# Conformer convolution's LayerNorm in two column ranges, with the latent range and the latent rows handled beside the first projection tile

## The chip, the cores and the metric

One NeuronCore of a Trainium2 chip runs the whole program. The metric is the device time of one execution in microseconds. Engines are named as in the profile: PE is TensorE (PEld its weight loads), DVE is VectorE, ACT is ScalarE, POOL is GpSimd, SP is the engine whose queue issues most of the DMAs.

## What is computed

A two-layer backbone over 256 context tokens and 512 latent tokens of width 1024. Layer 0 mixes tokens by a convolution module, layer 1 by windowed attention; each layer ends in a top-2 mixture of 16 experts. The change touches the end of layer 0's convolution module and the start of the step that follows it.

```python
def layernorm(x, g, b):
    x32 = x.astype(jnp.float32)
    mu = jnp.mean(x32, axis=-1, keepdims=True)
    xc = x32 - mu
    var = jnp.mean(xc * xc, axis=-1, keepdims=True)
    return (xc * lax.rsqrt(var + EPS) * g.astype(jnp.float32) + b.astype(jnp.float32)).astype(x.dtype)

def conformer_conv(h, pw1, pw1_b, dw, dw_b, ln_g, ln_b, pw2, pw2_b):
    u = h @ pw1 + pw1_b
    u = u[..., :D_MODEL] * jax.nn.sigmoid(u[..., D_MODEL:])
    half = (CONV_WIDTH - 1) // 2
    u = depthwise_conv(u, dw, dw_b, (half, half))
    u = jax.nn.silu(layernorm(u, ln_g, ln_b))
    return u @ pw2 + pw2_b
...
        xl = xl + mod_l[2] * yl
...
            xc = xc + mod_c[2] * yc
            hc2 = modulate(rmsnorm(xc, norm_ffn[i]), mod_c[3], mod_c[4])
            y2 = moe(jnp.concatenate([hc2, hl2], axis=1), *moe_prm)
```

`mod_l` and `mod_c` are the modulation vectors of the latent and the context stream: index 2 is the gate on the mixer's output, 3 and 4 are shift and scale of the norm before the experts.

## The kernel before, in words

**Layout.** The convolution's result lies transposed: `V` (storage AR) has the 1024 channels as 8 blocks of 128 partitions and, for each, `CONVW` = 783 columns: the 256 context tokens, some columns between, and the 512 latent tokens. The normalisation over channels is a sum over partitions and blocks, so PE makes it with a matrix of ones: the mean into `MEAN`, the sum of squares into `VAR` (both in PSUM).

**End of the convolution block** (lines 1360 to 1380 on DVE, 1278 to 1290 on ACT). DVE subtracts the mean (L1368), ACT squares each block (L1282), PE sums the squares (L1246). Then one chain runs over all 783 columns: DVE makes variance plus epsilon into `STD` (L1374), ACT takes the root (L1284), DVE the reciprocal (L1377), DVE multiplies each of the 8 blocks by it (L1380), and ACT applies Silu with the channel's gain and bias (L1287). Each Silu raises `z_ready`, on which the projection's matmuls wait (`wait0`).

`STD` has no storage of its own: it lies in row 3 of `ROWS`, a tile of six rows of 1024 numbers, broadcast to all partitions. Rows 0, 1, 2 are to hold the context stream's gate, scale and shift; rows 3, 4, 5 those of the latent stream. They are written by `load_row` (L468) out of `rows_of_layer`, a small array in HBM that is itself written late, by two DMAs (L464).

**Projection and routing** (`project_and_route`, from L751). Six tiles of 128 tokens, two of context and four of latents. For each tile PE makes two halves of 512 columns (`h` = 0, 1; L858, 8 channel blocks each, two instructions for a block). DVE multiplies a half by the gate row (L975) and adds it to the residual `X` (L978): `add_half`. Halves of `X` are then transposed by PE (L800) for the router, ACT and DVE take the squares' sum and the norm, DVE writes the scaled and shifted tile (L1048, L1053), and `choose` picks the experts. In program order PE asks for DVE's first half of tile `i` (`x_new`) before the transposes that stand after the fourth block of its second half. The bias of the projection times the gate is made once for each stream into `GB` (L1061, storage RING) and added to `X` ahead of the tile's halves (`bias_x`, L1037).

**Order of the queues.** Everything is written out by hand, in one list of instructions for each engine. SP's list at this place: the projection's bias row (L1157 to L1186 stand before it, the load of the second pointwise weights), the two writes of `rows_of_layer`, then a wait for `rows_out` and for all 8 products of L1380 (`scaled`), the six row loads, the first expert weights (L708), eight clearing writes of an output array (L782), and the tiles' results (L786). DVE waits for all six rows (`rows_in`) before it does anything of the projection.

```python
                sp.wait_ge(rows_out, 32)
                if L == 0:

                    sp.wait_ge(scaled, KT)
                for s in streams:
                    for v, w in zip((2, 4, 3), row[s]):
                        load_row(sp, L, s, v, w, rows_in[L])
```

Of the kernel before, what the change touches and what calls it, by code (L numbers as in the profile page):

```python
# [16 lines left out]
ALU = mybir.AluOpType  # L17
ACT = mybir.ActivationFunctionType
# [106 lines left out]
def build(nc, a, out):  # L125
    with ExitStack() as stack:
# [621 lines left out]
            st(V_.tensor_scalar(CUM[:, 0, :], const("iota")[:, 0:NE], float(deep), None, ALU.mult))  # L748
            dve_n[0] = st.n

        def project_and_route(block, L, lhs, weights, bias, tiles, lhs_wait):  # L751


            NT = len(tiles)
# [10 lines left out]
            @block.sync  # L765
            def _(sp):

                sp.wait_ge(rows_out, 32)
                if L == 0:

                    sp.wait_ge(scaled, KT)
                for s in streams:
                    for v, w in zip((2, 4, 3), row[s]):
                        load_row(sp, L, s, v, w, rows_in[L])
                load_weight(sp, L, 0, 1)
                load_weight(sp, L, 0, 3)
                if L == 1:
                    load_weight(sp, L, 1, 1)
                    load_weight(sp, L, 1, 3)
                sp.wait_ge(nil_set[L], 1)  # L780
                for b in range(MINB[L] // 2, MAXB[L] // 2):
                    sp.dma_start(yd[L][b * P:(b + 1) * P, :].rearrange("p (a n) -> p a n", a=4),  # L782
                                 NIL.unsqueeze(1).to_broadcast([P, 4, 256])).then_inc(nil_out[L], 16)
                for i in range(NT - 1):
                    sp.wait_ge(h2_ready[L], i + 1)
                    sp.dma_start(h2d[L][i * P:(i + 1) * P, :], H2[:, i % 2, :]).then_inc(h2_out[L][i % 2], 16)  # L786
                sp.wait_ge(y_summed[L], 2 * NT)
                sp.wait_ge(x_new[L], 2 * NT - 1)
                load_weight(sp, L, L + 1, 1)
                load_weight(sp, L, L + 1, 3)  # L790
                load_weight(sp, L, 0, 2)
                for b in range(2):
                    sp.wait_ge(h2_out[L][b], 16 * (NT // 2))
                sp.wait_ge(nil_out[L], 16 * (MAXB[L] - MINB[L]) // 2)

            @block.tensor
            def _(pe):
# [52 lines left out]
                for i in range(NT):  # L850
                    u = i - 1
                    for h in range(2):
                        if i >= 2:
                            pe.wait_ge(y_used[L], 2 * (i - 2) + h + 1)
                        for k in range(KT):
                            if i == 0 and h == 0:
                                lhs_wait(pe, k)
                            ins = pe.matmul(PS[:, 2 * (i % 2) + h, :], lhs(i, k),  # L858
                                            weights(k)[:, h * 512:(h + 1) * 512],
                                            start=(k == 0), stop=(k == KT - 1))  # L860
                            if u >= 0 and h == 0 and k == 1:
# [101 lines left out]
            def _(dve):  # L963
# [91 lines left out]
                if L == 1:  # L1055
                    router_tables(dve, L, streams)
                    st.n = dve_n[0]
                dve.wait_ge(rows_in[L], 16 * 3 * len(streams) + (16 if bias is not None else 0))
                if bias is not None:
                    for s in streams:  # L1060
                        st(V_.tensor_tensor(GB[:, s, :], bias, ROWS[:, row[s][0], :], ALU.mult))  # L1061
                    bias_x(0)
                for i in range(NT):
                    t = tiles[i]
                    u = i - 1
                    add_half(i, 0)
                    if i:
                        choose(u)
                    add_half(i, 1)
                    if i:  # L1070
                        read_rank(u)
                    dve.wait_ge(xB_turned[L], i + 1)
                    V_.tensor_copy(XTB[:, i % 2, 4:8, :], PS[:, 5, :].rearrange("p (k n) -> p k n", k=4)).then_inc(
                        xB_copied[L], 1)
                    dve.wait_ge(f_sq[L], 2 * i + 2)
                    V_.scalar_tensor_tensor(out=ss[:, t:t + 1], in0=ss_half[:, 0, t:t + 1], scalar=EPS,
                                            in1=ss_half[:, 1, t:t + 1], op0=ALU.add, op1=ALU.add).then_inc(f_ms[L], 1)
                    if i:
                        destinations(u, u + 1)
                    norm_scale(i)  # L1080
                    if i == 0:
                        dve.wait_ge(shift_summed[L], 1)
                        s0 = streams[0]
                        V_.tensor_copy(CST[:, s0:2, :],
                                       SHIFT[:, s0 * NE:2 * NE].rearrange("p (s e) -> p s e", e=NE)).then_inc(
                                           shift_ready[L], 1)
                        dve.wait_ge(shift_ready[L], 1)
                    scale_h2(i)
                    shift_h2(i)
                    if bias is not None and i < NT - 1:  # L1090
                        bias_x(i + 1)
                choose(NT - 1)
# [48 lines left out]
        BROW = RING[:, 0, 0:D]  # L1141
        GB = RING[:, 0, D:3 * D].rearrange("p (s n) -> p s n", s=2)
        STD = ROWS[:, 3, 0:CONVW]
        MEAN = PSF[:, 0:CONVW]
        VAR = PSF[:, 1024:1024 + CONVW]
        NSTEP = 2 * (1 + TAPS)
# [10 lines left out]
        with nc.Block() as block:  # L1157
# [93 lines left out]
            def _(act):  # L1251
# [26 lines left out]
                for f in range(KT):  # L1278
# [1 line left out]
                    if f >= 2:  # L1280
                        act.wait_ge(sq_used, f - 1)
                    nc.scalar.activation(SQ[:, f % 2, :], V[:, f, :], ACT.Square).then_inc(squared, 1)  # L1282
                act.wait_ge(var_ready, 1)
                nc.scalar.activation(STD, STD, ACT.Sqrt).then_inc(std_ready, 1)  # L1284
                for f in range(KT):
                    act.wait_ge(scaled, f + 1)
                    nc.scalar.activation(V[:, f, :], V[:, f, :], ACT.Silu,  # L1287
                                         scale=cols[:, VC["conv_ln_g"] + f:VC["conv_ln_g"] + f + 1],
                                         bias=cols[:, VC["conv_ln_b"] + f:VC["conv_ln_b"] + f + 1]).then_inc(z_ready, 1)

            @block.vector
            def _(dve):
# [78 lines left out]
                    mod_rows_copy(dve, L)  # L1371
                router_tables(dve, 0, (0, 1))
                dve.wait_ge(sq_used, KT)
                nc.vector.tensor_scalar(STD, VAR, 1.0 / D, EPS, ALU.mult, ALU.add).then_inc(var_ready, 1)  # L1374
                dve.wait_ge(std_ready, 1)
                st = Steps(dve, dve_step, dve_n[0])
                st(nc.vector.reciprocal(STD, STD))  # L1377
                for f in range(KT):
                    dve.wait_ge(centred, f + 1)
                    nc.vector.tensor_tensor(V[:, f, :], V[:, f, :], STD, ALU.mult).then_inc(scaled, 1)  # L1380
                dve_n[0] = st.n

            def lhs0(i, k):
                at = i * P if i < CT else LAT0 + (i - CT) * P
                return V[:, k, at:at + P]

            def wait0(pe, k):
                if k == 0:
                    pe.wait_ge(w_in[0], 32)
                pe.wait_ge(z_ready, k + 1)  # L1390

            project_and_route(block, 0, lhs0, lambda k: Wpw2[k // 4][:, k % 4, :], BROW, list(range(TILES)), wait0)


        def load_qkv(sp, c):
# [706 lines left out]
                        nc.scalar.activation(den[:, c], den[:, c], ACT.Exp).then_inc(sink_exp, 1)  # L2102


        def wait1(pe, k):
            if k == 0:
                pe.wait_ge(w_in[1], 32 + 64)
                pe.wait_ge(o_normed, 4 * (LT - 1) + 1)

# [6 lines left out]
        with nc.Block() as block:  # L2116
# [17 lines left out]
            @block.sync  # L2134
            def _(sp):
                o = out[0].rearrange("(t p) d -> t p d", p=P)
                for i, t in enumerate(lat):
                    sp.wait_ge(scaled, KT + i + 1)
                    sp.dma_start(o[i], X[:, t, :]).then_inc(out_sem, 16)
                sp.wait_ge(out_sem, 16 * LT)  # L2140

# [20 lines left out]
```

## Time and profile before

| | |
|---|---|
| median of 3 runs | 1592.72 us (1591.69 to 1592.96) |
| the profiled execution | 1593.22 us, span 1591.4 us |
| busy share of PE, DVE, ACT, POOL | 85%, 48%, 32%, 8% |
| mean granted TensorE clock | 0.927 of full speed |
| bytes moved by DMA | 342.97 MB, mean 216 GB/s |

A busy time is a sum over the span; it does not say which engine sets the pace at a given moment. The trace lists each instruction's start, its duration and, in brackets, how long its engine had been idle before it and whose result ended that idle time. Numbers are microseconds from the span's start unless marked ns. Names are those of the storage: AR is `V`, ROWS is the rows and `STD`, RING holds `GB`, the halves `YT` and the tile `H2`, PS is PSUM.

### The profile page before, as it was taken

What the parts mean: (1) busy time and instruction counts of PE and PEld (TensorE: products, weight loads), DVE (VectorE), ACT (ScalarE), POOL (GpSimd) and SP (SyncE); (2) the same over time, 40 slices, a digit from 0 to 9 for tenths busy, and PEclk for the clock granted to TensorE, in tenths of its full rate; (3) what the DMA queues carried; (4) which work ended last, traced back from release to release, by engine and by line L of the source; (5) the groups of instructions that cost most, each with busy time, mean ns of one, the idle gap of its engine ahead of it and who ended that gap; (6) DMA issues with size and microseconds to landing.
All of it is one profiled execution on the core that took longest, in us unless ns stands there. A gap on an engine that the chain in (4) does not pass through costs nothing. (4 is left out here: it accounts for less than half of the span.)

```text
span 1591.4 us, 22877 instructions
## 1 busy us (share of the span) xinstructions
PE 1360.1 (85%) x6778; PEld 638.4 (40%) x6779; DVE 757.1 (48%) x1405; ACT 508.5 (32%) x783; POOL 125.4 (8%) x176
## 2 busy tenths in 40 slices
PE   4799998469968899999998399799897779989980
PEld 2555563224433333333332244388643323323330
DVE  2699999955764221222211542366547322232215
ACT  4101001043324443343322320166422253454422
POOL 0000000001221000101000200000002100000001
PEclk9899999789978999999999699799998899999995
DMA  9825464535059999899642500130094799999915
GB/s 345 286 70 204 146 258 176 206 116 203 27 207 372 375 371 344 277 303 343 204 142 95 213 0 0 30 77 2 19 365 166 261 336 384 366 378 375 353 33 191
DMA packets 163826, 342.97 MB, mean 216 GB/s; under 512 B 9104, under 2 KB 34304, under 8 KB 163776
## 3 DMA queue, kind: packets, MB, share of 16 engines
q1 hardware_dynamic: 146448, 298.29, 52.8%
q0 software_dynamic: 7440, 25.43, 5.2%
q10 hardware_dynamic: 9888, 18.62, 3.4%
q8 instruction: 27, 0.44, 0.1%
q14 instruction: 23, 0.19, 0.0%
HBM read 312.06 MB, written 30.24 MB: 215 GB/s over the span
## 5 line engine op out<-in xcount | busy, mean ns | idle before, releaser
L1480 PE MATMUL PS<-WR,XT 128*64 128x512 f32 x1760 | 414.4, 614 | 36.2 <-DVE WR L1613 26.5
L1480 PEld LDWEIGHTS PS<-WR,XT 128*64 128x64 f32 x1760 | 127.6, 141 | 273.2 <-issue 208.8
L1625 DVE TENSOR_TENSOR HID<-PS,SIL 64x512 f32<-64x512 f32 x55 | 37.6, 683 | 396.9 <-ACT SIL L1557 396.9
L1493 PE MATMUL PS<-WR,HTT 128*64 128x512 f32 x880 | 206.6, 613 | 9.5 <-ACT HTT L1562 9.5
L1546 ACT ACTIVATE WR<-WR 128x2048 f32 x90 | 169.0, 1906 | 107.8 <-issue 96.7
L1198 PE MATMUL PS<-HT,RING 128*128 128x512 f32 (+1 forms) x512 | 170.1, 496 | 8.5 <-DVEq L1296 8.4
L1613 DVE COPY WR<-WR 128x2048 f32 x90 | 107.1, 1224 | 114.6 <-DMA WR<-in_moe_w 51.3
L1198 PEld LDWEIGHTS PS<-HT,RING 128*128 128x128 f32 x512 | 100.0, 196 | 76.3 <-issue 68.4
L1318 DVE SCALAR_TENSOR_TENSOR AR<-AR,cols 128x783 f32 (+3 forms) x135 | 126.5, 937 | 0.0
L1318 DVE SCALAR_TENSOR_TENSOR ROWS<-AR,cols,ROWS 128x783 f32<-128x783 f32 (+2 forms) x126 | 118.0, 936 | 0.0
L1493 PEld LDWEIGHTS PS<-WR,HTT 128*64 128x64 f32 x880 | 59.6, 140 | 111.5 <-issue 108.0
L858 PE MATMUL PS<-RING,AR 128*128 128x512 f32 x192 | 92.4, 624 | 9.3 <-ACT AR L1287 9.3
L1794 PE MATMUL PS<-RING,HT 128*128 128x512 f32 x224 | 98.7, 598 | 1.3 <-ACT ROWS L1831 1.3
L1557 ACT ACTIVATE SIL<-PS 64x512 f32<-64x512 f32 x55 | 32.7, 595 | 122.1 <-PE PS L1480 122.1
L2035 DVE CUSTOM_DVE_ANT_0 HT<-PS,AR 128x512 f32<-128x512 f32 (+1 forms) x64 | 49.8, 816 | 33.6 <-PE PS L1959 33.6
L1569 ACT ACTIVATE YO<-PS 128x512 f32<-128x512 f32 x55 | 32.3, 588 | 97.5 <-PE PS L1493 97.5
L1794 PEld LDWEIGHTS PS<-RING,HT 128*128 128x128 f32 x224 | 42.5, 193 | 52.3 <-issue 52.3
L424 PE MATMUL PS<-RING,sc 128*32 128x512 f32 x384 | 50.2, 652 | 14.4 <-DMA RING<-in_w_mod 9.3
L858 PE MATMUL PS<-RING 128*128 128x512 f32 x128 | 60.2, 614 | 2.5 <-PEq L1935 2.5
L713 POOL DMA_INDIRECT XG<-moe_in,icur x57 | 54.8, 962 | 42.7 <-POOL icur L1448 41.4
L1562 ACT ACTIVATE HTT<-PS 128x256 f32<-128x256 f32 x55 | 20.7, 376 | 109.9 <-issue 60.1
L1259 ACT ACTIVATE ROWS<-PS,cols 128x256 f32<-128x256 f32 (+1 forms) x16 | 9.3, 581 | 144.0 <-PE PS L1198 144.0
(234 smaller groups left out, 1337.5 us busy)
## 6 DMA issues: line engine op xcount, KB each, us to landing
WR<-in_moe_w SPq DMA_DIRECT2D x192, 1024.0 KB, 15.1
RING<-in_w_mod SPq DMA_DIRECT2D x24, 2048.0 KB, 15.0
moe_out<-YO ACTq DMA_DIRECT2D x110, 128.0 KB
RING<-in_conv_pw SPq DMA_DIRECT2D x16, 512.0 KB, 5.4
moe_out<-HT SPq DMA_DIRECT2D x16, 512.0 KB, 8.4
ROWS<-rows_of_layer SPq DMA_DIRECT2D x12, 512.0 KB, 6.1
RING<-in_attn_w_qkv SPq DMA_DIRECT2D x3, 2048.0 KB, 8.6
RING<-in_conv_pw SPq DMA_DIRECT2D x2, 2048.0 KB, 9.9
```

The source lines that it names most:

```text
L424: ins = pe.matmul(PS[g:g + 32, bank, :], sc2[:, k, :], w[:, k, :], start=(k < 4), stop=(k >= 4), tile_position=(0, g))
L713: pool.indirect_dma_start(out=XG[:, :], out_offset=None, in_=src, in_offset=bass.IndirectOffsetOnAxis(ap=icur[0:SUB, 0:1], axis=0)).then_i ...
L858: ins = pe.matmul(PS[:, 2 * (i % 2) + h, :], lhs(i, k), weights(k)[:, h * 512:(h + 1) * 512], start=(k == 0), stop=(k == KT - 1))
L1198: ins = pe.matmul(conv_bank(j, u, lat), PWB[:, j, u, k, :], HT[:, k, t0:t0 + n], start=(k == 0), stop=(k == KT - 1))
L1318: ins = nc.vector.scalar_tensor_tensor(out=to, in0=u, scalar=w, in1=to, op0=ALU.mult, op1=ALU.add)
L1480: ins = pe.matmul(PUV[g * SUB:(g + 1) * SUB, :], XT[:, k, :], w[:, k * FE:(k + 1) * FE], start=(k == 0), stop=(k == KT - 1), tile_position ...
L1493: ins = pe.matmul(PYO[c * SUB:(c + 1) * SUB, :], HTT[:, k, :], W2[:, at:at + 512], start=(k == 0), stop=(k == FE // P - 1), tile_position= ...
L1546: return nc.scalar.activation(to, src, ACT.Copy)
L1613: return nc.vector.tensor_copy(to, src)
L1625: nc.vector.tensor_tensor(HID[:, :], PUV[0:SUB, :], SIL[:, :], ALU.mult).then_inc(hid_ready[L], 1)
L1794: ins = pe.matmul(PS[:, bank, :], HT[:, k, t * P:(t + 1) * P], slot(QKV_SLOT[c], KT)[:, k, :], start=(k == 0), stop=(k == KT - 1))
L2035: nc.vector.tensor_tensor_reduce(out=SS[:, 2 * (s % 3) + b, 0:w], in0=PSF[:, 1024 * b:1024 * b + w], in1=mask, scale=-DH ** -0.5, scalar=n ...
```

## The change

`RANGES` cuts the 783 columns into the 256 of the context and the 527 that are left. The steps variance, root, reciprocal, product and Silu are issued for each range. DVE makes both variances, then reciprocal and products of the context range; the latent range's reciprocal (`invert(dve, 1)`) and products (`scale_v(1)`) are issued inside `project_and_route`, the former after the first `bias_x`, the latter between the two halves of tile 0. PE waits for the context range's Silu at tile 0 and for the latent range's at tile 2. SP fetches the context rows as soon as `rows_of_layer` is written, and the latent rows after the last product; DVE waits for the context rows at the start and for the latent rows at the end of tile 0, where `GB` of the latent stream is now made. The other waits on `scaled` are renumbered.

```diff
@@ project_and_route, SP
                 sp.wait_ge(rows_out, 32)
-                if L == 0:
-
-                    sp.wait_ge(scaled, KT)
                 for s in streams:
+                    if s == 1 and L == 0:
+
+                        sp.wait_ge(rows_in[L], 64)
+                        sp.wait_ge(scaled, 2 * KT)
                     for v, w in zip((2, 4, 3), row[s]):
                         load_row(sp, L, s, v, w, rows_in[L])
@@ project_and_route, PE
-                            if i == 0 and h == 0:
-                                lhs_wait(pe, k)
+                            if h == 0:
+                                lhs_wait(pe, i, k)
@@ project_and_route, DVE
-                dve.wait_ge(rows_in[L], 16 * 3 * len(streams) + (16 if bias is not None else 0))
+                dve.wait_ge(rows_in[L], 64 if bias is not None else 48)
                 if bias is not None:
-                    for s in streams:
-                        st(V_.tensor_tensor(GB[:, s, :], bias, ROWS[:, row[s][0], :], ALU.mult))
+                    st(V_.tensor_tensor(GB[:, 0, :], bias, ROWS[:, row[0][0], :], ALU.mult))
                     bias_x(0)
+                    dve_n[0] = st.n
+                    invert(dve, 1)
+                    st.n = dve_n[0]
                 for i in range(NT):
...
                     add_half(i, 0)
+                    if i == 0 and scale_v is not None:
+                        scale_v(1)
                     if i:
                         choose(u)
                     add_half(i, 1)
...
                     shift_h2(i)
+                    if bias is not None and i == 0:
+                        dve.wait_ge(rows_in[L], 112)
+                        st(V_.tensor_tensor(GB[:, 1, :], bias, ROWS[:, row[1][0], :], ALU.mult))
                     if bias is not None and i < NT - 1:
                         bias_x(i + 1)
@@ convolution block, ACT
-                act.wait_ge(var_ready, 1)
-                nc.scalar.activation(STD, STD, ACT.Sqrt).then_inc(std_ready, 1)
+                for q, (c0, c1) in enumerate(RANGES):
+                    act.wait_ge(var_ready, q + 1)
+                    nc.scalar.activation(STD[:, c0:c1], STD[:, c0:c1], ACT.Sqrt).then_inc(std_ready, 1)
+                for q, (c0, c1) in enumerate(RANGES):
+                    for f in range(KT):
+                        act.wait_ge(scaled, q * KT + f + 1)
+                        nc.scalar.activation(V[:, f, c0:c1], V[:, f, c0:c1], ACT.Silu,
...
+            def invert(dve, q):
+                c0, c1 = RANGES[q]
+                st = Steps(dve, dve_step, dve_n[0])
+                dve.wait_ge(std_ready, q + 1)
+                st(nc.vector.reciprocal(STD[:, c0:c1], STD[:, c0:c1]))
+                dve_n[0] = st.n
+
+            def scale_v(q):
+                c0, c1 = RANGES[q]
                 for f in range(KT):
...
+                    nc.vector.tensor_tensor(V[:, f, c0:c1], V[:, f, c0:c1], STD[:, c0:c1], ALU.mult).then_inc(scaled, 1)
@@ the projection's wait on its left operand
-            def wait0(pe, k):
-                if k == 0:
+            def wait0(pe, i, k):
+                if i == 0 and k == 0:
                     pe.wait_ge(w_in[0], 32)
-                pe.wait_ge(z_ready, k + 1)
+                if i in (0, CT):
+                    pe.wait_ge(z_ready, (0 if i < CT else KT) + k + 1)
```

DVE's instructions from the variance to the end of tile 0's second half, before (AR is `V`, ROWS is `STD` and the rows, RING<-RING,ROWS of 1024 columns is `GB`):

```order
L1374 TENSOR_SCALAR ROWS<-PS 128x783
L1377 RECIPROCAL ROWS<-ROWS 128x783
L1380 TENSOR_TENSOR AR<-AR,ROWS 128x783 x8
L962 UNCONDITIONAL_BRANCH
L1061 TENSOR_TENSOR RING<-RING,ROWS 128x1024 x2
L1037 TENSOR_TENSOR X<-X,RING 128x1024
L975 TENSOR_TENSOR RING<-PS,ROWS 128x512
L978 TENSOR_TENSOR X<-X,RING 128x512
```

and now (line numbers are those of the changed kernel):

```order
L1398 TENSOR_SCALAR ROWS<-PS 128x256
L1398 TENSOR_SCALAR ROWS<-PS 128x527
L1306 RECIPROCAL ROWS<-ROWS 128x256
L1312 TENSOR_TENSOR AR<-AR,ROWS 128x256 x8
L963 UNCONDITIONAL_BRANCH
L1061 TENSOR_TENSOR RING<-RING,ROWS 128x1024
L1038 TENSOR_TENSOR X<-X,RING 128x1024
L1306 RECIPROCAL ROWS<-ROWS 128x527
L976 TENSOR_TENSOR RING<-PS,ROWS 128x512
L979 TENSOR_TENSOR X<-X,RING 128x512
L1312 TENSOR_TENSOR AR<-AR,ROWS 128x527 x8
L976 TENSOR_TENSOR RING<-PS,ROWS 128x512
```

The latent reciprocal now stands ahead of tile 0's first half and the latent products behind it; one of the two `GB` products has left this place, and stands behind tile 0's shift (`L1097 TENSOR_TENSOR RING<-RING,ROWS 128x1024`), ahead of the bias of tile 1.

SP's list at the same place, before (WR is the expert weights' storage):

```order
L464 DMA rows_of_layer<-ROWS 96x128 [waits mod_rows] x2
L765 UNCONDITIONAL_BRANCH
L468 DMA ROWS<-rows_of_layer 128x1024 [waits scaled,rows_out]
L468 DMA ROWS<-rows_of_layer 128x1024 x5
L708 DMA WR<-in_moe_w 128x4x512 x4
```

and now:

```order
L464 DMA rows_of_layer<-ROWS 96x128 [waits mod_rows] x2
L765 UNCONDITIONAL_BRANCH
L468 DMA ROWS<-rows_of_layer 128x1024 [waits rows_out]
L468 DMA ROWS<-rows_of_layer 128x1024 x2
L468 DMA ROWS<-rows_of_layer 128x1024 [waits scaled,rows_in]
L468 DMA ROWS<-rows_of_layer 128x1024 x2
L708 DMA WR<-in_moe_w 128x4x512 x4
```

Three row loads no longer wait for a product; the other three, and the weights behind them, wait for the latent products.

## Rows read from the trace of the kernel before

**Rows 1.** The profile's page: engines' busy time, share and instructions.
```profile
PE 1360.1 (85%) x6778; PEld 638.4 (40%) x6779; DVE 757.1 (48%) x1405; ACT 508.5 (32%) x783; POOL 125.4 (8%) x176
```

**Rows 2.** Timeline of PE: start, us, engine, line, operation, count [idle before <-releaser].
```profile
338.84 13.36 PE L858 MATMUL PS<-RING,AR 128*128 128x512 f32 x24 [9.28 <-ACT AR L1287]
361.29 1.12 PE L800 MATMUL PS<-CN,X 128*128 128x128 f32 x4 [9.09 <-DVE X L978]
362.20 5.00 PE L858 MATMUL PS<-RING,AR 128*128 128x512 f32 x8
...
372.32 0.60 PE L800 MATMUL PS<-CN,X 128*128 128x128 f32 x4
...
382.77 3.60 PE L858 MATMUL PS<-RING,AR 128*128 128x512 f32 x8
```

**Rows 3.** Timeline of DVE, from the variance to tile 1.
```profile
329.67 0.97 DVE L1374 TENSOR_SCALAR ROWS<-PS 128x783 f32<-128x783 f32 x1 [3.88 <-PE PS L1246]
331.56 5.05 DVE L1377 RECIPROCAL ROWS<-ROWS 128x783 f32<-128x783 f32 x1 [0.92 <-ACT ROWS L1284]
336.65 7.16 DVE L1380 TENSOR_TENSOR AR<-AR,ROWS 128x783 f32<-128x783 f32 x8
356.04 2.48 DVE L1061 TENSOR_TENSOR RING<-RING,ROWS 128x1024 f32<-128x1024 f32 x2 [12.23 <-DMA ROWS<-rows_of_layer]
358.55 1.23 DVE L1037 TENSOR_TENSOR X<-X,RING 128x1024 f32<-128x1024 f32 x1
359.81 0.69 DVE L975 TENSOR_TENSOR RING<-PS,ROWS 128x512 f32<-128x512 f32 x1
...
372.96 0.69 DVE L1073 COPY HT<-PS 128x512 f32<-128x512 f32 x1 [4.31 <-PE PS L800]
...
376.87 1.22 DVE L1037 TENSOR_TENSOR X<-X,RING 128x1024 f32<-128x1024 f32 x1
378.95 0.69 DVE L975 TENSOR_TENSOR RING<-PS,ROWS 128x512 f32<-128x512 f32 x1 [0.86 <-PE PS L858]
```

**Rows 4.** Timeline of ACT, the root and the Silus.
```profile
330.68 0.85 ACT L1284 ACTIVATE ROWS<-ROWS 128x783 f32<-128x783 f32 x1 [1.50 <-DVE ROWS L1374]
331.55 1.28 ACT L1287 ACT_TABLE_LOAD   x1
337.66 7.56 ACT L1287 ACTIVATE AR<-AR,cols 128x783 f32<-128x783 f32 x8 [4.83 <-DVE AR L1380]
```

**Rows 5.** Timeline of SP's queue around the row writes and the row loads.
```profile
324.19 0.82 SPq L464 DMA_DIRECT2D rows_of_layer<-ROWS  x2
343.89 3.14 SPq L468 DMA_DIRECT2D ROWS<-rows_of_layer  x6
```

**Rows 6.** Source lines L464 (row writes, x2), then L468 (row loads, x12).
```profile
DMA to landing us min/median/max: 1.5/1.6/1.6
...
DMA to landing us min/median/max: 3.5/6.1/9.7
```

**Rows 7.** Stretches: start:end us, engines' busy us (count), granted clock, DMA share, GB/s.
```profile
329.50:334.00 4.50, 0.06 (x1) 0.00 (x0) 3.41 (x2) 2.14 (x2) 0.00 (x0) 1.00 0.00 0
...
338.80:344.00 5.20, 5.16 (x6) 2.19 (x7) 5.01 (x6) 5.20 (x6) 0.00 (x0) 0.50 0.01 3
...
361.30:365.00 3.70, 3.70 (x8) 2.15 (x9) 0.00 (x0) 2.66 (x5) 0.00 (x0) 0.50 1.05 388
```

**Rows 8.** Stretches: the projection's rest.
```profile
373.00:450.00 77.00, 77.00 (x298) 37.13 (x297) 59.82 (x195) 27.27 (x58) 20.74 (x16) 1.00 0.13 51
```

**Rows 9.** Stretches: PE after gaps of 2.5 and 2.7 us elsewhere.
```profile
289.60:293.00 3.40, 3.40 (x17) 0.68 (x17) 3.40 (x5) 0.00 (x0) 0.00 (x0) 0.55 0.00 0
...
1295.10:1299.00 3.90, 3.90 (x20) 1.36 (x20) 1.10 (x1) 1.92 (x1) 0.00 (x0) 1.00 1.02 351
```

**Rows 10.** Groups by shape: DVE and ACT operations of 527 and 256 columns.
```profile
L1353 DVE TENSOR_TENSOR AR<-AR,ROWS 128x527 f32<-128x527 f32 x1 | 0.7, 708 | 0.0
...
L621 ACT ACTIVATE HT<-HT,modc 128x256 f32<-128x256 f32 x3 | 1.8, 591 | 5.1 <-DVEq L450 5.1
```

More of the change, by code:

```diff
@@ L749, in router_tables, with project_and_route @@
             dve_n[0] = st.n
-        def project_and_route(block, L, lhs, weights, bias, tiles, lhs_wait):
+        def project_and_route(block, L, lhs, weights, bias, tiles, lhs_wait, invert=None, scale_v=None):
             NT = len(tiles)
@@ L1143, in build @@
         STD = ROWS[:, 3, 0:CONVW]
+        RANGES = ((0, CTX), (CTX, CONVW))
         MEAN = PSF[:, 0:CONVW]
@@ L1282, in _ @@
                     nc.scalar.activation(SQ[:, f % 2, :], V[:, f, :], ACT.Square).then_inc(squared, 1)
-                act.wait_ge(var_ready, 1)
-                nc.scalar.activation(STD, STD, ACT.Sqrt).then_inc(std_ready, 1)
+                for q, (c0, c1) in enumerate(RANGES):
[5 more added lines that the diff above has]
+                        nc.scalar.activation(V[:, f, c0:c1], V[:, f, c0:c1], ACT.Silu,
+                                             scale=cols[:, VC["conv_ln_g"] + f:VC["conv_ln_g"] + f + 1],
+                                             bias=cols[:, VC["conv_ln_b"] + f:VC["conv_ln_b"] + f + 1]).then_inc(z_ready, 1)
+            def invert(dve, q):
[6 more added lines that the diff above has]
+                c0, c1 = RANGES[q]
                 for f in range(KT):
[L1286 to L1289, printed above, removed]
+                    nc.vector.tensor_tensor(V[:, f, c0:c1], V[:, f, c0:c1], STD[:, c0:c1], ALU.mult).then_inc(scaled, 1)
             @block.vector
@@ L1373, in _ @@
                 dve.wait_ge(sq_used, KT)
[L1374 to L1381, printed above, removed]
+                for c0, c1 in RANGES:
+                    nc.vector.tensor_scalar(STD[:, c0:c1], VAR[:, c0:c1], 1.0 / D, EPS, ALU.mult, ALU.add).then_inc(
+                        var_ready, 1)
+                dve.wait_ge(centred, KT)
+                invert(dve, 0)
+                scale_v(0)
             def lhs0(i, k):
@@ L1385, in lhs0 @@
                 return V[:, k, at:at + P]
-            def wait0(pe, k):
-                if k == 0:
+            def wait0(pe, i, k):
+                if i == 0 and k == 0:
                     pe.wait_ge(w_in[0], 32)
-                pe.wait_ge(z_ready, k + 1)
-            project_and_route(block, 0, lhs0, lambda k: Wpw2[k // 4][:, k % 4, :], BROW, list(range(TILES)), wait0)
+                if i in (0, CT):
+                    pe.wait_ge(z_ready, (0 if i < CT else KT) + k + 1)
+            project_and_route(block, 0, lhs0, lambda k: Wpw2[k // 4][:, k % 4, :], BROW, list(range(TILES)), wait0,
+                              invert, scale_v)
         def load_qkv(sp, c):
@@ L2102, in _, with wait1 @@
                         nc.scalar.activation(den[:, c], den[:, c], ACT.Exp).then_inc(sink_exp, 1)
-        def wait1(pe, k):
-            if k == 0:
+        def wait1(pe, i, k):
+            if i == 0 and k == 0:
                 pe.wait_ge(w_in[1], 32 + 64)
@@ L2137, in _ @@
                 for i, t in enumerate(lat):
-                    sp.wait_ge(scaled, KT + i + 1)
+                    sp.wait_ge(scaled, 2 * KT + i + 1)
                     sp.dma_start(o[i], X[:, t, :]).then_inc(out_sem, 16)
```

## The prediction

> **What bounds the kernel now.** The page comes first: PE is busy 85% of the span, DVE 48% [rows 1]. So a change pays where it takes away idle time of PE, and nothing else counts much. PE's timeline then shows two stops at this place. It is idle for 9.28 us until the first Silu of the normalisation (start 338.84), makes 24 instructions, and is idle again for 9.09 us until DVE has added tile 0's first half to `X` (restart 361.29) [rows 2]. DVE's timeline says what stands behind each. The first stop is the chain variance, root, reciprocal (5.05 us), product, Silu over all 783 columns. The second is a wait of 12.23 us on the row loads: DVE is done with the products at 343.81 and gets its rows at 356.04; two `GB` products, the bias and the half follow, and only then may PE go on [rows 3]. SP's queue shows why the rows are late: `rows_of_layer` is written by DMAs issued from 324.19, but the loads are issued from 343.89, right after the last product [rows 5]. No DMA runs meanwhile (0 GB/s from 329.5 to 334) [rows 7]. Behind tile 0, PE is busy 77.00 of 77 us at the full granted clock [rows 8], so a microsecond won in tile 0 should be kept.
>
> **Step 1, the first stop gets shorter.** DVE starts at 329.67 as before. From 0.966 us for a product of 783 columns (8 in 7.16 us is 0.895 from start to start) [rows 3] and 0.708 for 527 columns [rows 10] I take 1.0 ns a column and 0.16 fixed: 0.43 us for 256. Two variances end near 330.8. The context root ran beside the second one. The reciprocal costs (5.05 - 0.16)/783 = 6.2 ns a column, so 1.76 us for 256 and 3.45 for 527. Context reciprocal: 330.8 to 332.6, instead of 336.6. From there to PE's start were 2.19 us (product 0.97, Silu 1.03, 0.19 of handing over) [rows 2, 3, 4]; now 0.43 + 0.59 (a 256-column activation with scale and bias) [rows 10] + 0.19 = 1.2. The table load of 1.28 us [rows 4] stands behind one more root (some 0.6 us) and ends near 332.7, before the first product at 333.0. PE starts at 333.8: **5.0 us** won. The Silus then come every 0.5 us and a block of the half takes PE 0.9, so they feed it.
>
> **Step 2, the second stop goes.** It goes only if nothing else is late, so I follow each.
> - Context rows: the writes land 1.6 us after issue, near 326.5; three loads follow by 328 and land 3.5 to 9.7 us after issue [rows 5, 6], at 337.5 in the worst case, more likely 333. DVE wants them at 332.6 + 8 x 0.35 = 335.4. The late end costs 2.1 us of DVE, of which the 0.9 of slack below takes a part: at most 1.2 for PE.
> - DVE: one `GB` product and bias x (1.24 each), then the latent reciprocal (3.45): free at 341.4.
> - PE's first half: 16 instructions at 0.43 are 6.9 us at the full clock, 13.7 at the half one. With the clock I assume in step 3 it is done near 342.3. So DVE is 0.9 us early. The half and its sum take 1.45: `X` is new at 343.8. PE, four blocks further (3.5 us), asks for it at 345.8: no stop.
> - The latent products, 8 x 0.62 = 5.0, run to 348.8. PE ends its second half at 345.8 + 0.6 (transposes) + 3.5 = 349.8, and only then DVE has something to do for it. 1.0 us of slack.
> - ACT makes the latent Silus behind the products, at some 0.73 us each (0.945 for 783 columns [rows 4], less 256 at 0.83 ns), until 350.3. Queued behind them are the squares and the copy of tile 0's transposed half, that PE wants near 357 in tile 1. They take 3.6 us: done by 354.
> So the **9.1 us** of the second stop go, at a price of nothing while those covers hold.
>
> **Step 3, the clock.** After each stop PE ran at the lower level: 338.8 to 344 and 361.3 to 365 both show 0.50 (1.2 GHz) [rows 7]. With the second stop gone its slow restart goes too. The transposes took 1.12 us there and 0.60 one tile on, and the 8 matmuls 5.00 against 3.60 [rows 2]: **1.9 us** won. The first restart stays open. The new gap is 4.2 us instead of 9.3, and the level was still full 4.5 us into the old one [rows 7]. Elsewhere a gap of 2.5 us ended in 0.55 and one of 2.7 us in 1.00 [rows 9], so both happen. Before, 5.6 slow microseconds cost 2.8; the other restart had 3.7. I take a slow stretch of 3.4 to 3.7 that begins soon after PE's start, which wins **1.1 us**; the ends are 0 (as slow as before) and 2.8 (never slow). The Trainium skill ("TensorE: Matmul & The Clock Gate", Part 1) adds that one and the same kernel shows 6, 11 or 14 slow matmuls from run to run. No run here shows that yet; by it this term should be expected to spread and not to be one number.
>
> **Step 4, the end of tile 0.** Between PE's restart and the second transposes of tile 0 lay 11.0 us (361.29 to 372.32) [rows 2], now 1.9 less; from 345.8 that gives 355, where it was 372.32. From DVE's copy (372.96) to the bias of tile 1 (376.87) were 3.9 us [rows 3]; DVE now comes to the new wait on the latent rows near 359.7. SP issues these rows from 348.9 to 350; they land at 359.7 if the last takes the longest time seen, 9.7, and near 356 at the median [rows 6], with the weights' DMAs behind them on the same queue, as they stood behind the six loads before. The `GB` product then delays bias and first half of tile 1 by 1.24 us, of which 0.86 us was idle time [rows 3]. The rest, 0.4 us, is ahead of nothing that PE waits for: its own request for this sum stands four blocks on. Cost nothing; if that cover were gone, 0.4.
> The expert weights and the clearing writes are issued 5 us later than before, by SP's list, though three rows lighter. The first is used 80 us on: no cost.
> At tile 2 PE has waits on the latent Silus, which were done 40 us before. Nothing.
>
> **Sum.** 5.0 + 9.1 + 1.9 + 1.1 = 17.1 us. The profiled execution took 1593.22 us, 0.5 above the median of the three runs. 1593.2 - 17.1 gives **1576.1 us**. The experts' stage behind starts its loads on the last half's sum, so it moves as a whole.
>
> **The rivals.**
> - *The clock of the first restart goes another way.* As slow as before: 16.0 won, 1577.2. Not slow at all: PE is through its first half at 340.7 and DVE (341.4) is 0.7 late, so 18 to 19 won, 1574.7. For both speak rows 9. I count these as parts of the forecast.
> - *DVE sets the pace of tile 0.* Its list there has 10 more instructions. If each costs its whole duration and not the start-to-start time, the context products cost 0.6 more and the latent ones 0.7 more, and DVE is ready near 350.2 instead of 348.8: PE loses 0.4, or 1.5 if it was never slow. With rows as late as the bound, 1.2 more. The time would be 1577 to 1578.5. Against it: the products ran at 0.895 from start to start. The Trainium skill ("VectorE: DVE Perf Modes", the section on the TRN2 errata) speaks for it: a fixed latency for each instruction that reads SBUF, and the advice to tile at 512 elements or more, which the 256-column range breaks. Its formula (N + 151)/0.96 gives 973 ns for 783 columns where the row has 966, so the trace agrees on the size of one instruction. Chance 0.12.
> - *The gain is given back behind tile 0.* A later stage that is paced by transfers, and not by the moment they were released, would take part of it. For it: DMA shares of 1.05 at 361 to 365 [rows 7]. Against it: 51 GB/s over the rest of the projection [rows 8] and no early issue that now stands still. Some 8 us kept: 1585. Chance 0.05.
> - *The wait is still there.* If the rows were not what DVE waited for, or if the early loads are held on SP, only step 1 stays, and PE meets its stop 5 us earlier: 1588 if DVE gets through 5 us sooner, 1593 if not. The order of SP's list speaks against it. Chance 0.03.
> - *Slower: the latent rows take the place of the old wait.* SP holds them until 8 more products are done, with four weight loads right behind, and DVE waits for them with all of tile 1 queued behind. They would have to land 17 us after 359.7, so 27 us after their issue, to eat the gain; every us beyond adds one us. A landing at 30 us gives 1596. The longest of 12 was 9.7 [rows 6]. Chance 0.03.
>
> **How the numbers follow.** The forecast with its clock variants has 0.77 and spans 1574.5 to 1577.5. With 1.5 us to either side for the median and for clocks of later stretches that fall elsewhere, and with the DVE case, it reaches 1572.5 to 1580. That holds 0.77 + 0.12, less some 0.07 for sizes that I have wrong. A measurement of this kernel can tell about 0.2%, 3.2 us, from no change. Faster by more: 0.77 + 0.12 + 0.05 and half of the fourth, 0.95. Within it: 0.03. Slower: 0.02, what the last rival has beyond 3 us.
>
> **What would show it.** PE's first projection matmul near 333.8 instead of 338.84, with an idle time of 4.2. No idle time of PE above 0.5 us from there to the end of the projection. DVE's `GB` product of the context with no wait on the rows. DVE waiting on PE, by about 1 us, before each half of tile 0. The second `GB` product without a wait. The second transposes of tile 0 near 355.2. Wrong would be: DVE idle on ROWS loads at either place, PE idle on DVE in tile 0, or a place after 450 us where the distance to the old trace shrinks.

## The result, and the profile after

The changed kernel takes 1574.12 us in the median of 4 runs (1570.44 to 1578.86), the kernel before 1592.8: a ratio of 0.9881, interval 0.9859 to 0.9903. Nine more executions in two later jobs had medians of 1573.62 (kernel before: 1593.7) and 1573.63 (kernel before: 1592.57), with ratios of 0.9871 (0.9852 to 0.989) and 0.987 (0.9852 to 0.9887). Forecast were 1576.1 and a range of 1572.5 to 1580. The profiled execution is the slowest of the four: 1578.86 us, span 1577.1.

PE in the changed kernel (start, us, engine, line, count, [idle before <-releaser]), against [rows 2]:

```profile
318.52 13.10 PE L1255 MATMUL PS<-AR,ones 128*128 128x512 f32 x32 [1.53 <-ACT AR L1291]
335.70 12.24 PE L859 MATMUL PS<-RING,AR 128*128 128x512 f32 x24 [4.08 <-ACT AR L1298]
347.77 0.60 PE L801 MATMUL PS<-CN,X 128*128 128x128 f32 x4
348.21 3.60 PE L859 MATMUL PS<-RING,AR 128*128 128x512 f32 x8
351.65 3.64 PE L846 MATMUL PS<-WRT,modc 128*128 128x16 f32 x32
355.14 1.96 PE L859 MATMUL PS<-RING,AR 128*128 128x512 f32 x4
356.94 0.60 PE L801 MATMUL PS<-CN,X 128*128 128x128 f32 x4
```

One idle time is left, 4.08 us where there were 9.28, and the second, 9.09 us, is gone. I measure by a distance that leaves out whatever happened ahead of this place, and call it the distance from here on: from the end of the last square's sum to tile 0's second transposes. Here it is 356.94 - (318.52 + 13.10) = **25.3 us**. Before it was 372.32 - 329.56 (PE's start at 338.84 less its idle time of 9.28) = **42.8 us** [rows 2]. So tile 0 gained 17.4 us.

DVE, against [rows 3]:

```profile
331.74 1.04 DVE L1398 TENSOR_SCALAR ROWS<-PS 128x256 f32<-128x256 f32 x2 [6.18 <-PE PS L1255]
332.71 1.75 DVE L1306 RECIPROCAL ROWS<-ROWS 128x256 f32<-128x256 f32 x1
334.50 2.77 DVE L1312 TENSOR_TENSOR AR<-AR,ROWS 128x256 f32<-128x256 f32 x8
337.19 1.21 DVE L1061 TENSOR_TENSOR RING<-RING,ROWS 128x1024 f32<-128x1024 f32 x1
338.44 1.23 DVE L1038 TENSOR_TENSOR X<-X,RING 128x1024 f32<-128x1024 f32 x1
339.70 3.45 DVE L1306 RECIPROCAL ROWS<-ROWS 128x527 f32<-128x527 f32 x1
344.61 0.69 DVE L976 TENSOR_TENSOR RING<-PS,ROWS 128x512 f32<-128x512 f32 x1 [1.46 <-PE PS L859]
345.34 0.69 DVE L979 TENSOR_TENSOR X<-X,RING 128x512 f32<-128x512 f32 x1
345.95 5.02 DVE L1312 TENSOR_TENSOR AR<-AR,ROWS 128x527 f32<-128x527 f32 x8
351.85 0.69 DVE L976 TENSOR_TENSOR RING<-PS,ROWS 128x512 f32<-128x512 f32 x1 [0.88 <-PE PS L859]
...
361.49 1.22 DVE L1097 TENSOR_TENSOR RING<-RING,ROWS 128x1024 f32<-128x1024 f32 x1
362.74 1.23 DVE L1038 TENSOR_TENSOR X<-X,RING 128x1024 f32<-128x1024 f32 x1
364.00 0.69 DVE L976 TENSOR_TENSOR RING<-PS,ROWS 128x512 f32<-128x512 f32 x1
```

No bracket names the row loads. DVE waits for PE before both halves of tile 0, by 1.46 and 0.88 us; the latent `GB` product (L1097) and tile 1's first half follow without a wait.

Why is the profiled execution then at 1578.9 and not at 1575.8, which is 17.4 below 1593.2? The sum of squares took 13.10 us here, 10.80 before. The stretches around it in the changed kernel (start:end, its us, busy times, granted clock, DMA share, GB/s) show it at less than the full clock. This sum lies ahead of every changed instruction:

```profile
318.00:331.60 13.60, 13.08 (x32) 6.84 (x32) 7.46 (x14) 7.75 (x9) 0.00 (x0) 0.81 0.35 98
```

The long form stood in four of the thirteen profiles taken from the changed kernel on (12.84 to 13.10 us); of the kernel before there is one profile, with the short form, so how often it had the long one isn't known. So tile 0's second transposes came 15.4 us earlier than before, not 17.4. Of these, most arrive at the end: PE restarts after a gap in layer 1 at 1254.94 before and at 1239.96 now, 15.0 us apart, and the spans differ by 14.3.

The medians say more than the distance: the changed kernel lies 18.7, 20.1 and 18.9 us below the kernel before in the three jobs, 1.3 to 2.6 us beyond 17.4. No profile shows where that comes from. From tile 0's second transposes to the end of the span it is 1219.1 us before (1591.4 - 372.32) and 1220.2, 1219.7 and 1219.5 us in three profiles of the changed kernel, but 1213.9 us in another kernel with the same instructions behind this place (the one with one more reciprocal, below). So the rest of the kernel differs by up to 6 us between these profiles, and the surplus stays unexplained within that.

### The profile page after: what moved, and what is told of

It reads as the page before. It is cut to its first block and busy times, and to the rows that moved or that the text cites. A ratio compares the mean times of both kernels' runs of the same rounds, so it can differ in the third digit from the quotient of the medians.

```text
span 1577.1 us, 22898 instructions
## 1 busy us (share of the span) xinstructions
PE 1363.6 (86%) x6778; PEld 638.7 (40%) x6779; DVE 757.9 (48%) x1415; ACT 510.7 (32%) x792; POOL 124.5 (8%) x176
## 5 line engine op out<-in xcount | busy, mean ns | idle before, releaser
L1503 PE MATMUL PS<-WR,XT 128*64 128x512 f32 x1760 | 419.8, 621 | 31.6 <-DVE WR L1636 22.3
L1817 PEld LDWEIGHTS PS<-RING,HT 128*128 128x128 f32 x224 | 42.8, 194 | 53.1 <-issue 53.1
```

The lines of the kernel that those rows point to most:

```text
L1503: ins = pe.matmul(PUV[g * SUB:(g + 1) * SUB, :], XT[:, k, :], w[:, k * FE:(k + 1) * FE], start=(k == 0), stop=(k == KT - 1), tile_position ...
L1817: ins = pe.matmul(PS[:, bank, :], HT[:, k, t * P:(t + 1) * P], slot(QKV_SLOT[c], KT)[:, k, :], start=(k == 0), stop=(k == KT - 1))
```

## The experiments

Every kernel was timed beside the kernel before in the same job. Times spread by up to 9 us between executions of one kernel, so where a microsecond or two is in question I read the distance defined above.

### The changed kernel once more

> The changed kernel once more, unaltered. The four runs so far lie between 1570.4 and 1578.9 us, where four runs of the kernel before span 1.3 us. Theory A (the spread is the granted clock, which falls at other moments in each execution): the new profile shows tile 0's start, relative to the last square's sum, and the sum of squares itself with other durations than 4.07, 12.24 and 13.10 us, and the times keep spreading by some 5 us or more. Theory B (the profiled run was an outlier): times within 2 us of 1574.

Median 1573.62 us (1572.01 to 1576.85). PE, in the new profile:

```profile
319.25 10.80 PE L1255 MATMUL PS<-AR,ones 128*128 128x512 f32 x32 [1.53 <-ACT AR L1291]
334.13 12.23 PE L859 MATMUL PS<-RING,AR 128*128 128x512 f32 x24 [4.08 <-ACT AR L1298]
346.20 0.60 PE L801 MATMUL PS<-CN,X 128*128 128x128 f32 x4
...
355.36 0.60 PE L801 MATMUL PS<-CN,X 128*128 128x128 f32 x4
```

Half of theory A holds. The sum of squares is back at 10.80 us and accounts for 2.3 us between two executions; tile 0 itself did not vary at all (4.08, 12.23, distance 25.3). Nor is the spread new: 15 executions of the kernel before in this job lay between 1590.69 and 1598.87. I had taken four close ones for its nature.

### The rows' part alone

```diff
                 sp.wait_ge(rows_out, 32)
-                if L == 0:
-                    sp.wait_ge(scaled, KT)
                 for s in streams:
+                    if s == 1 and L == 0:
+                        sp.wait_ge(rows_in[L], 64)
+                        sp.wait_ge(scaled, KT)
```

and the latent `GB` product at tile 0's end; the normalisation stays in one range of 783 columns.

> The kernel before with the rows' part of the change alone: context rows fetched early, latent rows behind the last product, the latent GB product at the end of tile 0; the normalisation stays in one range of 783 columns. By the prediction's steps: step 1 is lost and PE starts its first tile near 338.8 as before, DVE has finished bias and GB by 346.3, PE's first half is ready near 348.5, so the second stop (9.1 us) and its slow restart (1.9 us) go: 11.0 us below before, 1581.8 us. Rival (the two parts need each other): less than 5 us below before, because DVE is late with something else.

Median 1582.85 us (1579.59 to 1584.87), ratio 0.993 (0.9906 to 0.9955): 10.9 us below the kernel before, forecast 11.0. Distance 31.5 us, which is 11.3 less than 42.8. PE:

```profile
338.96 13.22 PE L859 MATMUL PS<-RING,AR 128*128 128x512 f32 x24 [9.29 <-ACT AR L1290]
352.01 0.60 PE L801 MATMUL PS<-CN,X 128*128 128x128 f32 x4
352.45 3.60 PE L859 MATMUL PS<-RING,AR 128*128 128x512 f32 x8
```

The first stop stands as before, the second and its slow restart are gone. DVE has no wait on the rows and is idle for 2.53 us until PE has made the first half (DVE's L976 at 348.85), so even here, with a late normalisation, PE sets the pace of the tile.

### The column ranges alone

```diff
                 invert(dve, 0)
                 scale_v(0)
+                invert(dve, 1)
+                scale_v(1)
```

with all six row loads behind `scaled` at `2 * KT`, and DVE waiting for all of them, as before.

> The two column ranges alone: all products are made before the projection (context range first), and all six rows are fetched behind the last product, as before. Theory: PE starts some 5 us earlier and stops 5 us earlier, since DVE's wait for the rows ends the same 12 us behind the last product, which itself comes about 0.6 us later than before: 0 to 1 us slower than before, 1593.4 us. Rival (step 1 is worth its 5.0 us by itself): 1588 us.

Median 1592.62 us of ten executions, ratio 0.9987 (0.9973 to 1.0001). One of the ten took 4849.04 us; nothing on record explains it, and the ratio leaves it out. Distance 42.8 us, that of the kernel before. PE and DVE:

```profile
333.71 12.23 PE L858 MATMUL PS<-RING,AR 128*128 128x512 f32 x24 [4.08 <-ACT AR L1290]
361.43 1.11 PE L800 MATMUL PS<-CN,X 128*128 128x128 f32 x4 [15.48 <-DVE X L978]
```

```profile
356.18 2.49 DVE L1061 TENSOR_TENSOR RING<-RING,ROWS 128x1024 f32<-128x1024 f32 x2 [12.48 <-DMA ROWS<-rows_of_layer]
```

PE starts 5.1 us earlier and then waits 15.48 us instead of 9.09. The 6.4 us that step 1 and the clock win go into the second stop, all of them. So by the distance the ranges are worth nothing alone and 6.2 us (31.5 - 25.3) on top of the rows, and the rows 11.3 alone.

### Keeping PE at work in the gap ahead of tile 0

```diff
                     ins.then_inc(sq_used, 1)
+                pe.wait_ge(w_in[0], 32)
+                for n in range(4):
+                    pe.matmul(PS[:, 6, :], ones[:, :], Wpw2[0][:, n, 0:512], start=True, stop=True)
```

> The changed kernel with four unused matmuls of 512 columns on PE in the gap ahead of tile 0 (into a PSUM bank nobody reads). They take 3.5 us at the full clock, the gap was 4.07 us. If the slow stretch of the first restart comes from this gap, tile 0's 24 instructions take about 10.4 us instead of 12.24 and the kernel is 1.5 to 2 us faster than the changed kernel in the same job, with less spread. Rival (the gap has no part in it, the clock falls anyway, or the extra matmuls hold up tile 0): same or slower.

Median 1574.95 us, ratio 0.9879 (0.9857 to 0.9901), beside 0.9871 for the changed kernel: no gain, and with 1570.37 to 1576.02 us no smaller spread either. PE tells why:

```profile
329.69 3.59 PE L1260 MATMUL PS<-RING,ones 128*128 128x512 f32 x8
333.93 10.54 PE L859 MATMUL PS<-RING,AR 128*128 128x512 f32 x24 [0.65 <-ACT AR L1301]
344.31 0.60 PE L801 MATMUL PS<-CN,X 128*128 128x128 f32 x4
344.74 3.60 PE L859 MATMUL PS<-RING,AR 128*128 128x512 f32 x8
348.18 3.64 PE L846 MATMUL PS<-WRT,modc 128*128 128x16 f32 x32
351.67 3.63 PE L859 MATMUL PS<-RING,AR 128*128 128x512 f32 x4
```

Tile 0 did get its 1.7 us (10.54 for 12.24). But four projection instructions behind the 32 narrow matmuls now take 3.63 us instead of 1.96. The stretches of this kernel put the clock beside it:

```profile
350.00:351.70 1.70, 1.70 (x18) 1.70 (x17) 0.00 (x0) 1.69 (x3) 0.00 (x0) 1.00 0.98 205
351.70:355.00 3.30, 3.30 (x6) 1.23 (x6) 0.00 (x0) 0.86 (x3) 0.00 (x0) 0.52 0.98 318
```

PE was busy without a break, and still the level fell. Whether that was chance is what a second profile of the same kernel was to tell.

> The kernel with four wide unused matmuls in the gap ahead of tile 0, once more. In its first profile tile 0 took 10.54 us and not 12.24, but the lower clock came later, right behind the 3.64 us of the 32 small shift matmuls (4 instructions 3.63 us and not 1.96), and the distance from the last square's sum to tile 0's second transposes stayed 25.2 us. Theory A (the small matmuls let the clock fall when they are not preceded by a slow stretch): the same again, 25.2 us. Theory B (it fell there by chance): 23.6 us.

It came out as theory A says: 10.54 us for tile 0, 3.64 us for the four instructions, distance 25.3, median 1575.07 us, ratio 0.9887 (0.9871 to 0.9904). That the fall repeats is shown by this; the reason that theory A gives for it is not.

### The shift matmuls in the gap

```diff
+                if L == 0:
+                    sum_shift()
                 for i in range(NT):
...
-                    if i == 0:
+                    if i == 0 and L == 1:
                         sum_shift()
```

> The changed kernel with PE's 32 small matmuls of the router's shift (3.64 us, between tile 0 and tile 1 so far) moved ahead of tile 0, into the gap of 4.08 us. Theory (PE sets the pace from its first projection matmul on): 3.6 us less from the last square's sum to tile 0's second transposes (25.3 us in both profiles of the changed kernel, 21.7 now), and about 1570 us. DVE would then wait some 1.5 us for ACT's second square, which stands behind the latent Silus, and that is covered by the time until PE asks for tile 1's first sum. Rival (tile 0 is already paced by DVE and ACT to within a microsecond): half of it or less, 1572 us.

Median 1570.71 us (1568.35 to 1571.72), ratio 0.9857 (0.9839 to 0.9875). PE, and DVE's one new wait:

```profile
329.17 3.64 PE L846 MATMUL PS<-WRT,modc 128*128 128x16 f32 x32
333.40 12.23 PE L861 MATMUL PS<-RING,AR 128*128 128x512 f32 x24 [0.60 <-ACT AR L1300]
345.91 5.32 PE L861 MATMUL PS<-RING,AR 128*128 128x512 f32 x12
351.06 0.61 PE L801 MATMUL PS<-CN,X 128*128 128x128 f32 x4
```

```profile
353.49 0.16 DVE L1083 SCALAR_TENSOR_TENSOR ss<-ss_half 128x1 f32<-128x1 f32 x1 [1.08 <-ACT RING L911]
```

Distance 21.7 us, as expected. The wait for ACT's square behind the latent Silus is there and costs nothing up to this point, but not all of the 3.6 us is kept. In tile 1 PE starts 0.2 us late at L832, whose weights waited for DVE's ranking of tile 0 (L1008):

```profile
361.53 3.60 PE L861 MATMUL PS<-RING,AR 128*128 128x512 f32 x8
365.20 0.39 PE L832 MATMUL PS<-HT,CN 128*128 128x16 f32 x2
```

and tile 1's second transposes come 16.4 us behind those of tile 0 (367.46), where the changed kernel has 16.05 (356.94 to 372.99). So 3.2 us are left. The gap before tile 0 shrank from 4.08 to 0.60 us and the tile takes the same 12.23 us with its slow stretch. For the same comparison in one job the two kernels ran again.

> The kernel with the shift matmuls in the gap once more, timed beside the changed kernel (next run). Expected: 3 to 3.6 us below it, as the distance in the trace says (21.7 against 25.3 us); the single times of both spread by some 5 us, so ten runs of each in all are compared.

> The changed kernel once more, as the base for the kernel with the shift matmuls in the gap: 1573 to 1575 us in the median.

1570.89 us (1567.64 to 1571.45) against 1573.63 (1570.08 to 1576.96): 2.7 us where 3 to 3.6 were expected, ratios 0.9852 (0.9839 to 0.9866) and 0.987 (0.9852 to 0.9887), whose intervals overlap. Over all jobs, nine executions of the one and thirteen of the other, the medians are 1570.89 and 1573.62, again 2.7 us. The distances are 21.7 and 25.3, as in the first job. In these two profiles the sum of squares had its long form, 13.02 and 12.84 us.

### How much time DVE has: one reciprocal more, and three

```diff
                     invert(dve, 1)
                     st.n = dve_n[0]
+                    for n in range(1):
+                        st(V_.reciprocal(H2[:, 1, 0:527], ROWS[:, 0, 0:527]))
```

and the same with `range(3)`.

> The changed kernel with one more reciprocal of 527 columns (3.45 us, into a part of the tile H2 that is overwritten later) on DVE behind the latent one. It tests the cover of step 2: DVE was 1.46 us early for the first half, and PE asks for its sum 1.75 us after it is there, 3.2 us together. Expected: 0.3 us more than 25.3 from the last square's sum to tile 0's second transposes. Rival (DVE sets the pace of tile 0): the whole 3.5 us, 28.8.

> The same with three such reciprocals, 10.4 us. Expected: PE stops at tile 0's first transposes for 10.4 - 3.2 = 7.2 us, and restarts at the lower clock, 1 to 2 us more: 33 to 34.5 us from the last square's sum to tile 0's second transposes, and the whole kernel 8 to 9 us slower than the changed one. This is the size of a stop that the changed kernel has taken away.

One: distance 25.7, 0.4 more. Three: 35.4, 10.1 more. The times are of single executions, 1571.41 and 1582.32 us, and can't carry this: the first is even below the changed kernel's median, because the rest behind tile 0 took 1213.9 us there (1214.2 us in the second) and not some 1220. PE with one, then with three:

```profile
346.45 0.66 PE L801 MATMUL PS<-CN,X 128*128 128x128 f32 x4 [0.20 <-DVE X L979]
```

```profile
354.39 1.12 PE L801 MATMUL PS<-CN,X 128*128 128x128 f32 x4 [7.17 <-DVE X L979]
355.30 5.88 PE L859 MATMUL PS<-RING,AR 128*128 128x512 f32 x8
```

The stop is 7.17 us, forecast 7.2, so DVE's cover of 3.2 us is right to about a tenth. The restart was under-costed: the transposes and 8 matmuls took 2.8 us more than at the full clock, not 1 to 2, and the distance of 35.4 us lies outside the expected 33 to 34.5.

### The latent rows behind the weights

```diff
                         sp.wait_ge(scaled, 2 * KT)
+                        load_weight(sp, L, 0, 1)
+                        load_weight(sp, L, 0, 3)
```

In layer 0 they no longer stand behind the rows.

> The changed kernel with the four first weight loads ahead of the latent row loads on SP: the slower rival's mechanism made to happen. The rows are then issued some 7 us later, behind 4 MB at 390 GB/s, and land near 367 in the frame in which DVE asked for them at 359.9. Expected: DVE waits about 7 us before the latent GB product, PE stops some 5 us in the second half of tile 1, and the kernel is 5 to 7 us slower than the changed one. Rival (the rows of one queue are not held up by what was issued ahead of them, or are slowed little): no wait, no difference.

1581.83 us, a single execution. DVE and PE:

```profile
367.34 1.22 DVE L1099 TENSOR_TENSOR RING<-RING,ROWS 128x1024 f32<-128x1024 f32 x1 [7.33 <-DMA ROWS<-rows_of_layer]
```

```profile
371.33 1.12 PE L803 MATMUL PS<-CN,X 128*128 128x128 f32 x4 [5.76 <-DVE X L981]
372.24 5.61 PE L861 MATMUL PS<-RING,AR 128*128 128x512 f32 x8
```

Tile 0 is untouched (25.3); in tile 1 DVE waits 7.33 us and PE stops for 5.76, and the restart is slow again: transposes and 8 matmuls take 1.12 and 5.61 us instead of 0.60 and 3.60, 2.5 us more. Together that is 8.3 us, more than the 5 to 7 expected, and again it is the restart that was left out. The path to the delay was also another than expected. The rows were not issued some 7 us later: their issue begins at 351.93, 2.4 us behind the first weight load's (349.50), and the three take until 356.1. Most of the delay is in the landing. The longest from issue to landing is 12.9 us in this trace; in the changed kernel it is 7.3:

```profile
DMA to landing us min/median/max: 3.6/5.8/7.3
```

### Wide matmuls in the earlier gap

The shift matmuls in their new place, and:

```diff
                 pe.sem_inc(mod_summed[1], 1)
+                for n in range(17):
+                    pe.matmul(PS[:, 2, :], ones[:, :], ones[:, 0:1].to_broadcast([P, 512]), start=True, stop=True)
```

> The same with 17 unused matmuls of 512 columns on PE in the 17 us in which it waits for the last tap of the convolution. If the gap is what makes PE restart at the lower clock at 313.6 (mean sum 2.98 us there, 1.56 us for the block before), the mean sum takes 1.7 us, the sum of squares never shows 13.1 us, and the kernel is 1.3 us (up to 3.5 in an execution with the long form) faster than without them. Rival: the matmuls run over the gap at the lower clock and hold up the mean sum: slower.

Median **1568.52 us** (1566.47 to 1569.83), ratio 0.9845 (0.9831 to 0.9858), the fastest kernel of the study: 2.4 us below the same one without them in the same job, where 1.3 were expected. The single times overlap (1567.64 to 1571.45 without them), so what is shown of the cause is the mean sum's part, 1.4 us:

```profile
294.08 16.58 PE L1249 MATMUL PS<-ones 128*128 128x512 f32 x34
313.20 1.58 PE L1233 MATMUL PS<-AR,ones 128*128 128x512 f32 x4 [1.22 <-DVE AR L1366]
```

The last block's mean sum takes 1.58 us instead of 2.98, and DVE's last tap is still what it waits for, so the extra matmuls held up nothing. The sum of squares took 10.80 us; one profile can't show that the long form never comes.

## Why the prediction was right

- **Step 1**, 5.0 us: 5.2 (the idle time 9.28 became 4.08). The context reciprocal took 1.75 us where 1.76 was worked out, the latent one 3.45 for 3.45, the 8 context products 2.77 for 2.8.
- **Step 2**, 9.1 us: 9.1. The covers that DVE needed held: it was early by 1.46 and 0.88 us where 0.9 and 1.0 were worked out. The reading that the rows, and not the normalisation, made the second stop is shown from both sides: the ranges alone gave 0, the rows alone 11.3, which is the 9.1 and the slow restart behind it.
- **Step 3**, the slow restart that goes, 1.9: transposes and 8 matmuls took 1.12 and 5.00 us [rows 2] and take 0.60 and 3.60, so 1.9. The open one, 1.1: 24 instructions took 13.36 us from start to the stop, and 12.07 now until the transposes, so 1.3. The prediction gave this term a spread from 0 to 2.8. That it came out near 1.1 is in part luck: the rows named there [rows 9] pointed both ways, and the length of the slow stretch was an estimate. In all seven profiles with the idle gap of 4.08 us tile 0's instructions took 12.23 or 12.24 us, so it did not spread at all; the spread of the times comes in part from the sum of squares ahead, which the prediction doesn't have. The Trainium skill's statement ("TensorE: Matmul & The Clock Gate", Part 1) that the number of slow matmuls varies from run to run of a kernel is borne out there (10.80 and 13.10 us for the same 32 instructions), and not at tile 0.
- **Step 4**, nothing: nothing. The latent rows were there when DVE came to them. One cover in this step was misread. The latent Silus were said to be done 40 us before tile 2 asks for them; they end at 352.5 and tile 2's first instruction runs at 371.19, so it is 19 us, and about 19 also by the prediction's own times. It was still enough.
- **The sum**, 17.1: 17.4 by the distance. The time, 1576.1: 1574.1 and 1573.6 in the medians, so 18.7 to 20.1 us below the kernel before. The steps account for 17.4 of these. The 1.3 to 2.6 us beyond them have no cause on record.
- **The rivals.** *DVE sets the pace of tile 0* did not come true, and its price was wrong. The prediction let PE lose time as soon as DVE was late for the second half (349.8). But PE asks for that sum only in tile 1, after the shift matmuls and two blocks, at 356.94, and DVE had it ready at 353.3. With one reciprocal more DVE had no idle time before either half, and the loss was 0.4 us. The caution on small tiles that the Trainium skill gives ("VectorE: DVE Perf Modes", the TRN2 errata) costs something real on DVE, where the two ranges' products take 2.77 and 5.02 us and the one range's 7.16 [rows 3], 0.6 us more, but not where the kernel waits. The *slower* rival's mechanism was made to happen and is real: rows that land late stop PE, at the price of the delay beyond DVE's slack and a slow restart on top. It lacked its condition, since the rows landed in 7.3 us at the most. *Given back behind tile 0* took about 1 us in one profile, which can't be told from the spread.

## What to carry to other kernels

A wait in a queue that guards one tile often holds everything that shares its list. Here one wait, there because a scratch vector lay in a row that was to be loaded, delayed three loads whose own targets were free for 18 us (issued at 343.89 before, from 325.99 now). Of the other three only the gate's row is the scratch vector's own, row 3; the two beside it could have gone early too, which no run tried. Split the wait by what each transfer really overwrites before shortening the work in front of it: the shortened chain alone gained nothing here.

For the price of a delay, find the instruction at which the pacing engine asks for the result, not the moment at which the result could be ready. And look whether a gap that is left can take real work from behind it: 3.6 us of small matmuls fitted into one of 4.1.

## What the runs showed of the hardware

PE's busy time does not say that its clock is kept. In the kernel with the shift matmuls in the gap, PE is busy 3.50 of 4.10 us ahead of tile 0, with matmuls of 16 columns, and the level falls within the tile's first 0.6 us. In the changed kernel, where the same time is idle, it falls soon after the start too (tile 0 starts at 335.70, and the granted clock is 1.00 until 336.70 and 0.65 in the next half microsecond). The 24 instructions take 12.23 and 12.24 us. The stretches of the kernel with the shift matmuls in the gap:

```profile
329.30:333.40 4.10, 3.50 (x33) 3.43 (x32) 3.93 (x7) 3.08 (x5) 0.00 (x0) 1.00 0.70 227
333.40:334.00 0.60, 0.60 (x1) 0.27 (x2) 0.60 (x3) 0.60 (x2) 0.00 (x0) 0.73 0.00 0
334.00:335.00 1.00, 1.00 (x3) 0.36 (x2) 1.00 (x4) 1.00 (x3) 0.00 (x0) 0.50 0.00 0
```

With wide matmuls in the same gap the tile takes 10.54 us, and the level falls behind the narrow ones at the tile's end (0.52 at 351.7 to 355.0); both profiles of that kernel have the four slow instructions there. In the changed kernel the same narrow matmuls, at 351.65, are followed by four instructions at the full clock (1.96 us). The profiles differ in what went before: in all nine in which these matmuls stand between tile 0 and tile 1 and tile 0 had a slow stretch, the four instructions took 1.96 us; in the two in which it had none, 3.63 and 3.64. So the slow stretch was moved and not removed. Why, the runs don't say.
